# A two-layer encoder on one core: moving and re-homing the small operations that finish each attention unit

## The reference

```
A (8 heads): softmax(q k^T * 64**-0.5) v, q and k normalised per head and rotated, 2 k/v heads shared
B (4 heads): softmax((qn kn^T + qr kr^T) * 96**-0.5) v, low-rank q, k and v
C (4 heads): p_i = softmax(q_i k_i^T * 32**-0.5 - slope * |i - j|), i = 0, 1;  a = p_0 - lam * p_1;  a v
             then rmsnorm over the head and a factor
x = x + concat(o_a, o_b, o_c) @ w_out
```

## Time and profile before

| | us |
|---|---|
| runs, median (lowest to highest) | 3246.41 (3244.54 to 3246.54) |
| the profiled execution's own time | 3244.24 |
| span in its trace, first to last instruction | 3242.4 |
| PE busy, mean granted clock | 3017.4, 0.971 |
| DVE busy | 2086.2 |
| ACT busy | 1340.3 |
| POOL busy | 442.7 |

### The profile page before, as it was taken

One profiled execution on the slowest core, in us unless ns is written; L12 is line 12 of the kernel. 1 busy time (PEld: TensorE's weight loads), 2 busy tenths in 40 slices (PEclk: granted clock), 3 DMA queues, 4 the chain that ended last, 5 costly groups with the idle time before them and its releaser, 6 DMA issues.

```text
span 3242.4 us, 40207 instructions
## 1 busy us (share of the span) xinstructions
PE 3017.4 (93%) x13560; PEld 2320.5 (72%) x13560; DVE 2086.2 (64%) x2453; ACT 1340.3 (41%) x1837; POOL 442.7 (14%) x229
## 2 busy tenths in 40 slices
PE   6997988998999999999989888899989999999997
PEld 5685743676778888888867665357767788888886
DVE  5775788786255565555666668878842665656556
ACT  3224777786241222222323267778832322122214
POOL 3111122111410000000121112212124000000002
PEclk8998999999999999999989989999999999999998
DMA  5353322332121112111135433223221111111112
GB/s 174 133 162 104 89 58 50 75 82 85 40 65 40 52 39 65 39 52 39 39 114 178 149 82 73 62 58 78 59 98 46 52 52 52 52 39 50 53 39 65
DMA packets 269393, 237.80 MB, mean 73 GB/s; under 512 B 67648, under 2 KB 236352, under 8 KB 269248
## 3 DMA queue, kind: packets, MB, share of 16 engines
q1 hardware_dynamic: 269248, 235.99, 26.2%
HBM read 185.09 MB, written 50.86 MB: 73 GB/s over the span
## 4 chain that ended last, share of the span: by engine, by line
PE 73%; issue 12%; DVE 7%; ACT 4%; POOL 3%; DMA 1%; SPq 0%; ACTq 0%; DVEq 0%; POOLq 0%
PE ps L1579 27%; PE ps L1594 14%; PE ps L1348 12%; PE ps L1447 7%; PE ps L1494 4%; PE ps L1470 2%; ACT prob L833 2%; DVE ptl L1186 2%; PE ps L1475 1%; PE ps L1474 1%; PE ps L1564 1%; POOL prob L632 1%; ACT pth L865 1%; POOL rstd L589 1%; DVE ps L1137 1%
## 5 line engine op out<-in xcount | busy, mean ns | idle before, releaser
L1447 PE MATMUL ps<-stack 128*128 128x512 f32 (+1 forms) x1152 | 345.5, 421 | 76.2 <-ACT prob L833 61.5
L833 ACT ACTIVATE prob<-ps,nmx 128x1024 f32<-128x1024 f32 x320 | 356.6, 1114 | 69.5 <-DVE nmx L1141 32.2
L1266 DVE TENSOR_TENSOR xT<-ps,xT 128x512 f32<-128x512 f32 x352 | 241.1, 690 | 203.8 <-PE ps L1594 203.5
L1494 PEld LDWEIGHTS ps<-cst,prob 128*128 128x128 f32 x2048 | 238.8, 141 | 181.7 <-DVE ptl L1186 64.2
L1494 PE MATMUL ps<-cst,prob 128*128 128x128 f32 x2048 | 319.5, 279 | 33.0 <-DVE ptl L1186 27.2
L1186 DVE TENSOR_TENSOR ptl<-ps,pth 128x512 fp32r<-128x512 f32 x384 | 260.5, 687 | 117.9 <-ACT pth L865 113.9
L1447 PEld LDWEIGHTS ps<-stack 128*128 128x128 f32 (+1 forms) x1152 | 211.1, 195 | 172.0 <-ACT prob L833 115.4
L600 POOL TENSOR_TENSOR w0l<-wraw,w0h 128x1024 fp32r<-128x1024 f32 x34 | 84.5, 2489 | 1611.6 <-ACT w0h L712 1611.6
L1348 PE MATMUL ps<-xgh,w0h 128*128 128x512 f32 x768 | 252.7, 411 | 35.6 <-POOLq L231 10.1
L1231 DVE SCALAR_TENSOR_TENSOR cv<-u,vec,cv 128x1024 f32<-128x1024 f32 x176 | 225.9, 1283 | 90.8 <-ACT cv L938 80.4
L1579 PE MATMUL ps<-xgh,w0h 128*128 128x512 f32 x704 | 274.1, 389 | 2.4 <-ACT sq L930 2.4
(11 more groups left out here) (195 smaller groups left out, 5685.2 us busy)
## 6 DMA issues: line engine op xcount, KB each, us to landing
wraw<-in_w_up SPq DMA_DIRECT2D x88, 512.0 KB, 4.6
draw<-in_w_down SPq DMA_DIRECT2D x22, 1024.0 KB, 5.1
wraw<-in_w_in SPq DMA_DIRECT2D x36, 512.0 KB, 4.1
stack<-ka_d SPq DMA_DIRECT2D x64, 256.0 KB, 5.6
vst<-v_d SPq DMA_DIRECT2D x48, 256.0 KB, 3.8
x_d<-xT SPq DMA_DIRECT2D x2, 4096.0 KB, 18.3
qa_d<-rg SPq DMA_DIRECT2D x16, 512.0 KB, 2.7
wraw<-in_w_out SPq DMA_DIRECT2D x16, 512.0 KB, 5.4
```

The source lines that it names most:

```text
L833: act.activation(two(dst), ps[:, 2 * (i % 2):2 * (i % 2) + 2, :], ACT.Exp, bias=nmx[:, b, i:i + 1], scale=scale, accum_out=rsum[:, b, i:i ...
L1266: ins = dve.tensor_tensor(xs, ps[:, 4 + j % 4, :], xs, ALU.add)
L1447: ins = pe.matmul(ps[:, 2 * (i % 2) + kh, :], st[q][0:rows, c0:c0 + P], st[k][0:rows, kh * HALF:(kh + 1) * HALF], start=n == 0, stop=n == ...
L1494: ins = pe.transpose(ps[:, 4 + s % 2, m * P:(m + 1) * P], prob[:, b, m, s * P:(s + 1) * P], ident)
```

## The change

Four operations are put one step later: copy_part from 2 to 3 (and behind the copy of that step, since it stands after it in the step), sum_output from 3 to 4, hi_mix and copy_norm from 6 to 7 (again behind that step's copy). In groups A and B hi_mix no longer exists on ACT: POOL writes the product of `osum` and `nrm` twice, once rounded to `xgh` and once in place, and then subtracts. Group C keeps hi_mix on ACT.

```diff
@@ scale_output, on POOL
                     pool.wait_ge(norm_copied, l * NU + x["u"] + 1 + N_CREDIT)
+                    pool.tensor_tensor(mix_at(xgh, x), osum[rows, :], nrm[rows, :], ALU.mult).then_inc(mix_hi, 1)
                     pool.tensor_tensor(osum[rows, :], osum[rows, :], nrm[rows, :], ALU.mult).then_inc(o_ready, 1)
@@ act_unit, on ACT
-                        if s == 2 and prev:
+                        if s == 3 and prev:
                             copy_part(prev)
                         if s == 3 and nx and nx["group"] == "C":
                             scale_map(nx)
-                        if s == 6 and prev:
+                        if s == 7 and prev and prev["group"] == "C":
                             hi_mix(prev)
-                        if s == 6:
+                        if s == 7:
                             copy_norm(x)
@@ after the last unit, on ACT
                 copy_part(last)
-                hi_mix(last)
@@ dve_unit, on DVE
-                        if s == 3 and prev:
+                        if s == 4 and prev:
                             sum_output(prev)
```

## The result

The changed kernel took 3258.39 us (median of six runs: five of 3255.68 to 3260.18, and one of 3400.66 at a granted clock of 0.867, which the comparison leaves out), the kernel before on the same chip 3246.47 us (3242.22 to 3249.55). The ratio is 1.0035, with a 95% interval of 1.0022 to 1.0048: slower by 0.35%, some 11.9 us. The profiled execution took 3256.09 us, its span is 3254.3, also 11.9 above that of before.

The account below looks back on a forecast made before the run. PE, busy 3017.4 of 3242.4 us, was taken as the bound, so only added PE waits count. A 0, B 3.6, C 5.9, borders 3.8 and end 1.0 sum to 14.3 us, giving 3260 us, range 3244 to 3270.

Parts of the forecast that it names:

- ScalarE's gain 0: A and B units: hi_mix leaves ACT 48 times, but PE waits for none of what stands behind it; 0 us.
- Group A 0: Steps 3 to 7: copy 3 earlier, copy 4 later, PE's 0.55 us wait stays; 0, bounds -0.23 and +0.1 a unit.
- Group B +0.30 a unit: u1 to u6: later copy 4 delays PE's transposes of step 7 by 0.30 us a unit, 3.6 us in all.
- Group C +0.65, nine short units, 5.9: u9 to u14: sum_output behind the second mixing delays item 6's maximum 0.65 us in nine of 12 units, 5.9 us.
- The block: Group C: L1154 on DVE is held until POOL's addition ends; 5.9 us with it, 2.3 by plain durations.
- Borders +3.8: u7 and u8: later POOL addition, sum_output and POOL's three operations add 0.2 and 1.7 us, 3.8 in two layers.
- The end +1.0: After each phase's last unit: POOL makes one more product, +0.5 us, twice, 1.0 us.
- the first: Rival: freed ACT pulls the chain forward, A's wait goes (-16.5 us) and C costs 0; 3238 us, chance 0.10.
- The third: Rival: added waits in C drop PE below full clock in more units, 7.9 us more; 3268.5 us, chance 0.13.

Follow-up runs that it names:

- e1: Kernel before with POOL making the high half in groups A and B and hi_mix gone there from ACT, all steps as before: 3241.94 us, ratio 0.9984.
- i1: Kernel before with hi_mix and copy_norm in step 7 instead of 6, the high part staying on ACT: 3241.55 us, ratio 0.9988.
- g1: Changed kernel with copy_part and sum_output back in steps 2 and 3, POOL's product and step 7 kept: 3234.92 us, ratio 0.9962 to the kernel before.
- e4: Changed kernel with copy_part back in step 2, sum_output staying in step 4: 3245.14 us, ratio 0.9999 to the kernel before.
- e2: Kernel before with sum_output alone moved from step 3 to 4: 3259.56 us, ratio 1.0040.
- h1: Changed kernel with sum_output alone back in step 3, copy_part staying in step 3: 3227.21 us, ratio 0.9944 to the kernel before.
- h2: Changed kernel with sum_output back in step 3 and scale_map ahead of copy_part in step 3: 3235.40 us, ratio 0.9961 to the kernel before.
- i3: Kernel before with copy_part in step 3 and hi_mix and copy_norm in step 7, high part staying on ACT: 3230.22 us, ratio 0.9954.
- i2: Kernel before with copy_part alone moved from step 2 to step 3, behind that step's copy: 3234.01 us, ratio 0.9963.

## Why the prediction was right, and where it was not

3260 us was forecast, 3258.4 measured; the direction, the range and the place of most of it (sum_output in B and C) hold. The sum's closeness (14.3 us forecast for the two phases, 13.6 measured) is in part luck: A, B and the units u15 to u17 cost 7.4 us more than I had put down, C, the borders and the end 8.1 less.

1. *ScalarE's gain 0.* Wrong in size. e1 gives 0.16%, some 4 to 5 us, and i1 0.12%. ACT's busy share was the wrong thing to look at: hi_mix and copy_norm stood ahead of copy 7, and in the units before C and at the end of the phase everything waits for that copy (ACT 1.66 us, DVE 1.87). With product and step 7 together it is 12 us in the kernel before (g1) and 14 with sum_output in step 4 (e4 against e2), so this was the largest term that I left out.
2. *Group A 0.* The mechanism came out as written for this order of operations, to 0.1 us: copy 3 early, copy_part and copy 4 at 0.62 each, a wait of 0.49 on low part 4, the norm delayed. The size was +0.15 us in each of u18 to u30, 3.8 in all, above my upper bound of 0.1. The step that failed is the distance from sum_output to the maximum behind it: I took 0.61 from the row at 667.94, which stands behind a low part; behind sum_output it measured 0.71 (685.04 to 685.75, and 350.88 to 351.59). And the gain on low part 3 is not lost to copy_part's new place, as the sum reads, but to sum_output's: h1 keeps it.
3. *Group B +0.30 a unit.* Measured 0.39 (171.95 - 167.24, by 12), the same 0.1. PE waits 0.21 (predicted 0.3) before the transposes of step 7.
4. *Group C +0.65, nine short units, 5.9.* The block was right: L1154 ends with POOL's addition in both orders, and the mixing to maximum distance grew by 0.84 (predicted 0.7). In the Trainium skill, "SBUF — State Buffer", section "Who interferes with whom", a DVE instruction with two SBUF inputs contends with a GpSimd instruction that reads SBUF, and the order of issue decides which of the two blocks. The trace agrees, 0.93 us against 0.22 unblocked, and h1 and h2 show it on either engine. So these two engines also meet inside an instruction: the hold shows in its duration and not as a wait ahead of it. The group's sum grew by 4.0 in place of 5.9, but that is two terms. Units at a granted clock of 1.00 average 20.00 us before (six of them) and 20.59 after (ten of them), so the order costs 0.59 a unit, near the 0.65; in all twelve that would be 7.0, an estimate. Three units before ran at 0.93 to 0.94 and took 21.13 to 21.63 us; after, one took 22.04 us at 0.96, and it and the next share the low stretch. So by the same estimate the clock gave some 3 us back in this pair of profiles, which I had not forecast. What takes up the rest of the 0.84 on its way from DVE to PE I did not trace.
5. *Borders +3.8.* Wrong in sign, -0.7. I had counted what is added in u7 and u8 and not that copy 7 of u7 comes out from behind hi_mix and copy_norm, which i1 shows to be worth 0.98 us a layer in u7 alone. The delay by copy_part and sum_output is there too: e4 has 18.8 and 23.2 for the pair where after has 19.6 and 24.7 on average. The -0.7 itself is uncertain: PE's clock in the four border units is 0.82 to 1.00 before and 0.83 to 0.95 after, and u7 alone differs by 0.7 us between the layers of the kernel before.
6. *u15 to u17, +2.5,* were left out: the last C unit and the first A unit have the same two chains (17.17 to 17.75, and 12.57 to 13.23). A term per kind of unit should be counted over all units in which the chain stands.
7. *The end +1.0.* POOL's own part did grow by 0.50 us, from the first product to the end of the subtraction (3.32 us before, 2371.37 to 2374.69; now 3.82, 2385.02 to 2388.84), but it starts 5.56 us behind the last norm instead of 6.48, since the last copy no longer stands behind hi_mix: -0.7 in the two layers.

In the last unit of layer 1, POOL after, beside the earlier trace rows:

```profile
2385.02 1.26 POOL L619 TENSOR_TENSOR xgh<-osum,nrm 64x512 fp32r<-64x512 f32 x1 [1.66 <-DVE osum L1176]
...
2387.58 1.26 POOL L626 TENSOR_TENSOR xgl<-osum,xgh 64x512 fp32r<-64x512 f32 x1
```

Of the rivals, the first (3238 by ScalarE's pace) named the right mechanism for another kernel: A's wait does go when copy_part moves, and h1 and i3 gain by it, but only with sum_output in step 3. The third, that PE's clock would fall in more C units, did not come: its mean over the span is 0.971 before and 0.973 after, and in C it is low in fewer units after (item 4). By h1 (0.9944) and after (1.0035) the change is +30 us for sum_output in step 4 and -18 us for all the rest. The parts don't add up singly: sum_output costs 13 us in the kernel before (e2) and 30 behind the other edits, and copy_part behind copy 3 gains 12 us with sum_output in step 3 (i2) and costs 12 by the ratios with it in step 4 (e4 to after). They share one chain: copy_part's gain exists only while low part 3, sum_output and low part 4 stand in this order. The units bear it out: u18 to u31 of the two layers grow by 3.1 us from the kernel before to e2, and by 19.1 from h1 to after.

What stays open: why single C units of the changed kernel are 0.6 us longer than their neighbours at full clock, as u12 of layer 0 (21.13 against 20.45). DVE there (PE's granted clock is 1.00 from 498 to 503):

```profile
498.85 1.23 DVE L1137 CUSTOM_DVE_ANT_0 ps<-ps,dtab 128x1024 f32<-128x1024 f32 x1
...
500.83 1.23 DVE L1137 CUSTOM_DVE_ANT_0 ps<-ps,dtab 128x1024 f32<-128x1024 f32 x1 [0.46 <-issue]
```

The maximum of item 7 starts 1.98 us behind that of item 6 and shows 0.46 us in which it waited for nothing that the profile names, where in u11 it is 1.56 (478.15 to 479.71). In which units this and PE's lower clock fall differs from profile to profile, so a sum over C is uncertain, by an estimate of some 2 us a layer from the C sums above.

## What to carry over

Before an operation is moved by a step, write down on each engine what stands behind it in the new place, and whether PE waits for that within the same unit; the engine's busy share says nothing about it. A small operation belongs where its engine would otherwise wait: hi_mix, copy_norm and copy_part behind the copy that others wait for, but sum_output ahead of low part 4, in the time in which DVE would wait for copy 4. A cheap test is to move each of the operations alone and then with its neighbours in the chain, since their worths don't add up: the best kernel here was the change with one of its four moves taken back. Take start-to-start distances from a row with the same pair of operations, and count a term in every unit that has the chain, the border units too.

## What the runs showed of the hardware

- A PSUM copy of half the partitions on ACT (copy_part, 0.59 us) stands 0.62 us from its neighbours on both sides, while two full copies follow each other at 0.49 (1.09 for two in the earlier trace rows): the smaller operation is the dearer one in the queue there. (Ahead of scale_map it is 0.50, 428.24 to 428.74 in h1.)
- In the changed kernel DVE's maximum (L1139) starts 0.71 or 0.72 us behind sum_output of A and B in all 40 places, in the kernel before 0.60 to 0.65 behind a low part in all 84, though both last 0.69. It isn't a fixed distance of the pair: in the changed kernel 16 of 30 maxima stand 0.71 to 0.73 behind a low part, and C's maximum (L1137) starts 0.61 behind sum_output of B (428.87 to 429.48 in h1). What separates the two distances no run here tests.
- Which of two SBUF users is stretched depends on who issues first: POOL's product took 2.25 us in h1 (1.27 alone), where DVE's mixing was first, and the mixing took 2.27 us in h2 (1.28 alone), where one of POOL's products was first.
